# Two expert layers: 32-row transposes for the gathered rows, and heavy and light expert pairs in another order

## What is computed

```python
def hier_moe(h, w_rg, b_rg, w_re, b_re, w_g, w_u, w_d):
    ...
    g_prob = jax.nn.softmax((x @ w_rg + b_rg).astype(F32), axis=-1)
    g_p, g_i = lax.top_k(g_prob, 1)
    ...
    e_v, e_i = lax.top_k(e_sel, MOE_TOPK)
    gate = jax.nn.softmax(e_v, axis=-1) * g_p
    expert = g_i * MOE_PER_GROUP + e_i
    combine = jnp.sum(jax.nn.one_hot(expert, N_EXPERTS, dtype=F32) * gate[..., None], axis=1)
    hid = jax.nn.silu(jnp.einsum('nd,edf->nef', x, w_g)) * jnp.einsum('nd,edf->nef', x, w_u)
    hid = hid * combine[:, :, None].astype(hid.dtype)
    y = hid.reshape(B * T, N_EXPERTS * D_EXPERT) @ w_d.reshape(N_EXPERTS * D_EXPERT, D)
```

## Time and profile before

| | |
|---|---|
| three runs | 1136.48, 1138.15, 1139.21 us; median 1138.15 |
| the profiled execution | 1136.14 us, of which the traced span is 1134.3 us |
| PE busy | 1002.4 us (88%) |
| DVE, ACT, POOL busy | 520.5, 207.2, 123.0 us |
| chain that ended last | PE 70%, DMA 17%, DVE 5% |
| mean granted PE clock | 0.903 |
| moved by DMA | 304.67 MB, mean 269 GB/s |
| first expert loop | about 289 to 580 us |
| second expert loop | about 808 to 1097 us |

### The profile page before, as it was taken

How to read it: one execution, slowest core, us unless ns; L and a number is a source line. 1 busy time by engine, 2 the same in 40 slices (tenths; PEclk the granted TensorE clock), 3 DMA queues, 4 the chain that set the end, 5 groups by cost and what they waited for, 6 DMA issues and landing times.

```text
span 1134.3 us, 17810 instructions
## 1 busy us (share of the span) xinstructions
PE 1002.4 (88%) x6824; PEld 602.0 (53%) x6824; DVE 520.5 (46%) x1237; ACT 207.2 (18%) x428; POOL 123.0 (11%) x196
## 2 busy tenths in 40 slices
PE   3799999998999999988788988896899999988960
PEld 1355455453766667654544565344567666655630
DVE  1356442245354454434445557245444545532454
ACT  2223232121111111101122134011111111101111
POOL 2300111203110100100001000200201001000000
PEclk9899999997899999898979999996798999987795
DMA  9962445758787669999999440204867777999931
GB/s 313 368 250 75 156 151 198 290 183 348 276 325 296 275 238 386 420 418 419 417 385 347 145 139 7 79 19 161 350 261 290 297 297 305 418 420 419 419 132 55
DMA packets 78198, 304.67 MB, mean 269 GB/s; under 512 B 11512, under 2 KB 11824, under 8 KB 52648
## 3 DMA queue, kind: packets, MB, share of 16 engines
q1 hardware_dynamic: 66072, 277.08, 62.4%
q0 software_dynamic: 10768, 21.78, 5.6%
q10 hardware_dynamic: 1280, 4.72, 1.1%
HBM read 317.10 MB, written 5.32 MB: 284 GB/s over the span
## 4 chain that ended last, share of the span: by engine, by line
PE 70%; DMA 17%; DVE 5%; SPq 3%; ACT 2%; issue 1%; POOL 0%; ACTq 0%; DVEq 0%
PE psum L723 15%; DMA ring<-in_w_exp_up 13%; PE psum L1060 13%; PE psum L1014 11%; PE psum L1025 7%; PE psum L1082 5%; PE psum L795 4%; PE psum L921 4%; SPq L444 3%; PE psum L747 2%; DMA ring<-in_w_in_odd 2%; DMA ring<-in_w_mod 2%; PE psum L969 1%; PE psum L1191 1%; PE psum L819 1%
## 5 line engine op out<-in xcount | busy, mean ns | idle before, releaser
L1874 DVE TENSOR_TENSOR ht<-ht,psum 128x512 f32<-128x512 f32 x276 | 172.9, 681 | 173.0 <-PE psum L1025 172.8
L1060 PE MATMUL psum<-ring,arena 128*32 128x256 f32 x2816 | 174.7, 404 | 32.2 <-DMA ring<-in_w_exp_up 16.0
L1014 PEld LDWEIGHTS psum<-ident,arena 128*128 128x128 f32 x736 | 178.4, 334 | 23.0 <-issue 23.0
L1014 PE MATMUL psum<-ident,arena 128*128 128x64 f32 x736 | 185.1, 407 | 3.2 <-issue 3.2
L723 PE MATMUL psum<-ring,ht 128*128 128x512 f32 (+1 forms) x432 | 168.9, 548 | 3.4 <-ACT ht L1259 2.7
L1060 PEld LDWEIGHTS psum<-ring,arena 128*32 128x32 f32 x2816 | 96.2, 117 | 123.7 <-issue 54.2
L723 PEld LDWEIGHTS psum<-ring,ht 128*128 128x128 f32 x432 | 80.8, 190 | 84.3 <-issue 76.3
L1082 PE MATMUL psum<-ring,arena 128*32 128x512 f32 x704 | 93.8, 654 | 0.0
L1025 PE MATMUL psum<-y_top,to_token 64*128 64x512 f32 x276 | 89.5, 580 | 4.1 <-DVE y_low L1910 4.0
L1025 PE MATMUL psum<-y_low,to_token 64*128 64x512 f32 x276 | 78.8, 513 | 0.0
L1901 DVE TENSOR_TENSOR arena<-arena,psum 64x256 f32<-64x256 f32 x44 | 18.2, 413 | 123.6 <-ACT arena L1405 123.6
(11 more groups left out here) (319 smaller groups left out, 906.0 us busy)
## 6 DMA issues: line engine op xcount, KB each, us to landing
ring<-in_w_exp_gate SPq DMA_DIRECT2D x32, 2048.0 KB, 14.4
ring<-in_w_exp_up SPq DMA_DIRECT2D x32, 2048.0 KB, 16.9
ring<-in_w_exp_down SPq DMA_DIRECT2D x32, 2048.0 KB
ring<-in_w_mod SPq DMA_DIRECT2D x24, 2048.0 KB, 16.9
ring<-in_w_in_even SPq DMA_DIRECT2D x5, 2048.0 KB, 21.6
shift_scale<-mod_rows POOLq DMA_DIRECT2D x3, 2048.0 KB, 11.3
ring<-in_w_in_odd SPq DMA_DIRECT2D x3, 2048.0 KB, 20.0
ring<-in_w_out_even SPq DMA_DIRECT2D x2, 2048.0 KB, 8.9
```

The lines of the kernel that those rows point to most:

```text
L1014: t = pe.matmul(psum[:, 0, 2 * SLOTS * k:2 * SLOTS * (k + 1)], XS[v][:, k:D:KC], both_sides, start=True, stop=True)
L1060: mm = pe.matmul(psum[to:to + SLOTS, 2, 0:256], XT[:, k, SLOTS * e:SLOTS * (e + 1)], RG[:, 3 * u + a, e, k, :], start=(k == 0), stop=(k == ...
L1874: dve.tensor_tensor(acc, acc, bank(BACK_BANKS[c]), ALU.add).then_inc(M("added"), 1)
```

## The change

Four edits:

* **Transposes.** `turn_rows` uses, instead of 8 ordinary products of 128 rows with a 128 x 64 selection of the identity, 16 transposes of 32 rows each: for each of 8 column sets one transpose for rows 0 to 31 into bank 0 and one for rows 96 to 127 into bank 1 (`X_BANKS`). The input tile has its two experts apart, and `x_copy` reads two half banks.
* **Banks.** Since bank 1 is taken, `BACK_BANKS` becomes (6, 3, 7, 5, 6, 3): block 2 of `combine` writes the banks of block 0. Its first product now waits for addition 0, its second for addition 1, and VectorE does additions 0 and 1 ahead of the copy of the hidden transposes. Two waits at the start of the attention layer follow.
* **Table.** `in_slot` is written with both sides beside one another (128 columns instead of 64), so each table needs six products instead of twelve.
* **Order.** `IN_TURN` orders the pairs: two heavy, then four times a light and a heavy, then six light. VectorE computes table columns and the order of the pairs accordingly.

```diff
+IN_TURN = [True, True] + [False, True] * (HEAVY - 2) + [False] * (LIGHT - HEAVY + 2)
+PASS_LIST = [(place, part, heavy) for place, heavy in enumerate(IN_TURN) for part in range(1 + heavy)]
...
-BACK_BANKS = (6, 3, 1, 7, 5, 6)
+BACK_BANKS = (6, 3, 7, 5, 6, 3)
+X_BANKS = (0, 1)
...
-        XT = vx(KC * 2 * SLOTS, "p (k s) -> p k s", k=KC)
+        XT = vx(KC * 2 * SLOTS, "p (e k s) -> p e k s", e=2, k=KC)
...
-                    for side in range(2):
-                        rows = slice(2 * SLOTS * side, 2 * SLOTS * (side + 1))
-                        mm = pe.matmul(psum[rows, 7, 0:2 * PLACES], in_slot[:, i, :], in_pair[:, i], start=(i == 0), stop=(i == 5))
+                    mm = pe.matmul(psum[:, 7, 0:2 * PLACES], in_slot[:, i, :], in_pair[:, i], start=(i == 0), stop=(i == 5))
...
                     for k in range(KC):
-                        t = pe.matmul(psum[:, 0, 2 * SLOTS * k:2 * SLOTS * (k + 1)], XS[v][:, k:D:KC], both_sides, start=True, stop=True)
+                        for n, side in zip(X_BANKS, (slice(0, SLOTS), slice(3 * SLOTS, 4 * SLOTS))):
+                            t = pe.transpose(psum[:, n, SLOTS * k:SLOTS * (k + 1)], XS[v][side, k:D:KC], ident[side, side])
...
-                                if b == NB - 1 and part == 0 and n == 1:
-                                    pe.wait_ge(M("added"), q * 6 + 13)
+                                if b == NB - 1 and part == 0:
+                                    pe.wait_ge(M("added"), q * 6 + (13 + n))
...
-                    heavy = p < 2 * HEAVY
-                    place = p // 2 if heavy else p - HEAVY
+                    place, part, heavy = PASS_LIST[p]
                     u = place % 2
-                    new_weights = not heavy or p % 2 == 0
+                    new_weights = part == 0
...
-                    last_of_pair = p >= 2 * HEAVY or p % 2 == 1
+                    place, part, heavy = PASS_LIST[p]
+                    last_of_pair = part == int(heavy)
...
-                dve.tensor_scalar(is_heavy, rank_t, float(HEAVY), None, ALU.is_lt)
...
-                link(dve.scalar_tensor_tensor(slot_c, place_a, float(HEAVY), place_b, ALU.add, ALU.add))
+                dve.scalar_tensor_tensor(heavy_base, i64, float(PASSES - 2), h32, ALU.mult, ALU.add)
...
+                link(dve.tensor_tensor(slot_c, place_a, place_b, ALU.add))
...
-                link(dve.tensor_tensor(against, along_cols(rank), along_rows(iota16), ALU.is_equal))
+                dve.tensor_scalar(turn, rank, 2.0, -1.0, ALU.mult, ALU.add)
...
+                link(dve.tensor_tensor(against, along_cols(turn), along_rows(iota16), ALU.is_equal))
...
-                    add_half(q - 1, 0)
+                    for c in range(2):
+                        add_half(q - 1, c)
...
-                    for c in range(1, 6):
+                    for c in range(2, 6):
                         add_half(q - 1, c)
```

More of the change, by code:

```diff
@@ L117 @@
 FRONT = len(MOD_GROUPS["front"])
-MOD_BANKS = {"even": (4, 4), "gate": (0, 1), "scale": (2, 3), "norm_1": (5, 3), "router": (2, 3), "places": (2, 3), "norm_2": (2, 3),
+MOD_BANKS = {"even": (4, 4), "gate": (0, 1), "scale": (2, 3), "norm_1": (5, 3), "router": (2, 3), "places": (2, 3), "norm_2": (2, 7),
              "attention": (2, 3), "norm_3": (0, 1)}
@@ L357, in build @@
         Y_LO = rounded_at("y_low", 512)
-        in_slot = vx(6 * 2 * SLOTS, "p (i s) -> p i s", i=6)
+        in_slot = vx(6 * P, "p (i s) -> p i s", i=6)
         SGM = [vx(256, parts=2 * SLOTS) for _ in range(2)]
@@ L378, in build @@
         ef, odd, slot_p, slot_c = vx(6), vx(6), vx(6), vx(6)
-        rank_t, is_heavy, place_a, place_b = (vx(6) for _ in range(4))
+        rank_t, heavy_base, light_at, place_a, place_b = (vx(6) for _ in range(5))
+        turn, turn_tmp = vx(PAIRS), vx(PAIRS)
         n_max, n_light, n_rounds, n_tmp, n_tmp2 = vx(1), vx(1), vx(1), vx(5), vx(5)
@@ L994, in experts @@
                 for i in range(6):
-                    for side in range(2):
-                        rows = slice(2 * SLOTS * side, 2 * SLOTS * (side + 1))
-                        mm = pe.matmul(psum[rows, 5, 0:4], in_slot[:, i, :], in_first[:, i, :], start=(i == 0), stop=(i == 5))
+                    mm = pe.matmul(psum[:, 5, 0:4], in_slot[:, i, :], in_first[:, i, :], start=(i == 0), stop=(i == 5))
                 mm.then_inc(S("routing_ps"), 1)
@@ L1002, in experts @@
                 for i in range(6):
-                    for side in range(2):
-                        rows = slice(2 * SLOTS * side, 2 * SLOTS * (side + 1))
-                        mm = pe.matmul(psum[rows, 7, 0:2 * PLACES], in_slot[:, i, :], in_pair[:, i], start=(i == 0), stop=(i == 5))
+                    mm = pe.matmul(psum[:, 7, 0:2 * PLACES], in_slot[:, i, :], in_pair[:, i], start=(i == 0), stop=(i == 5))
                 mm.then_inc(S("routing_ps"), 1)
-                both_sides = ident[:, :].rearrange("p (a s) -> p a s", a=4)[:, 0:4:3, :]
                 def turn_rows(q, v):
@@ L1059, in one_pass @@
                                 to = 2 * SLOTS * (1 - a) + SLOTS * e
-                                mm = pe.matmul(psum[to:to + SLOTS, 2, 0:256], XT[:, k, SLOTS * e:SLOTS * (e + 1)], RG[:, 3 * u + a, e, k, :],
+                                mm = pe.matmul(psum[to:to + SLOTS, 2, 0:256], XT[:, e, k, :], RG[:, 3 * u + a, e, k, :],
                                                start=(k == 0), stop=(k == KC - 1))
@@ L1107, in _ @@
             mod_products(gate)
-            pe.wait_ge(S("moe0_added"), last * 6 + 14)
+            pe.wait_ge(S("moe0_added"), last * 6 + 15)
             mod_sum(gate)
@@ L1393, in x_copy @@
                     act.wait_ge(M("x_ps"), q + 1)
-                    act.copy(XT.rearrange("p k s -> p (k s)"), bank(0)).then_inc(M("x_sb"), 1)
+                    act.copy(XT.rearrange("p e k s -> p e (k s)"), psum[:, X_BANKS[0]:X_BANKS[1] + 1, 0:KC * SLOTS]).then_inc(M("x_sb"), 1)
                 def one_pass(r, p):
@@ L1791, in across @@
                     return iota[:, 0:n].rearrange("p (i n) -> p i n", i=1).broadcast_to([P, 6, n])
-                dve.tensor_tensor(in_slot, across(2 * SLOTS), along(slot_p, 2 * SLOTS), ALU.is_equal)
+                sides = [P, 6, 2, 2 * SLOTS]
+                dve.tensor_tensor(in_slot.rearrange("p i (e n) -> p i e n", e=2),
+                                  iota[:, 0:2 * SLOTS].rearrange("p (i e n) -> p i e n", i=1, e=1).broadcast_to(sides),
+                                  slot_p.rearrange("p (i e n) -> p i e n", e=1, n=1).broadcast_to(sides), ALU.is_equal)
                 link(dve.tensor_tensor(in_first, across(4), along(slot_c, 4), ALU.is_equal))
@@ L1819, in experts @@
                 link(a)
-                dve.tensor_scalar(is_heavy, rank_t, float(HEAVY), None, ALU.is_lt)
[L1821 to L1824, removed]
-                link(dve.scalar_tensor_tensor(slot_c, place_a, float(HEAVY), place_b, ALU.add, ALU.add))
+                dve.scalar_tensor_tensor(heavy_base, i64, float(PASSES - 2), h32, ALU.mult, ALU.add)
+                dve.tensor_scalar(place_a, rank_t, 3.0, -1.0, ALU.mult, ALU.add)
+                dve.tensor_scalar(place_b, rank_t, float(HEAVY), None, ALU.add)
+                link(dve.tensor_scalar(light_at, rank_t, 3.0, float(4 - 3 * HEAVY), ALU.mult, ALU.add))
+                dve.scalar_tensor_tensor(place_a, place_a, 0.0, heavy_base, ALU.max, ALU.add)
+                link(dve.tensor_tensor(place_b, light_at, place_b, ALU.min))
+                link(dve.scalar_tensor_tensor(place_b, h32, float(PASSES), place_b, ALU.mult, ALU.add))
+                link(dve.tensor_tensor(place_a, place_a, place_b, ALU.subtract))
+                link(dve.scalar_tensor_tensor(place_a, rank_t, float(HEAVY), place_a, ALU.is_lt, ALU.mult))
+                link(dve.tensor_tensor(slot_c, place_a, place_b, ALU.add))
                 dve.wait_ge(S("router_exp"), l + 1)
@@ L1863, in experts @@
                 dve.scalar_tensor_tensor(tab[:, 1, :], tab[:, 1, :], unused, tab_tmp, ALU.max, ALU.add).then_inc(S("table_ready"), 1)
-                link(dve.tensor_tensor(against, along_cols(rank), along_rows(iota16), ALU.is_equal))
+                dve.tensor_scalar(turn, rank, 2.0, -1.0, ALU.mult, ALU.add)
+                link(dve.tensor_scalar(turn_tmp, rank, 2.0, float(2 - 2 * HEAVY), ALU.mult, ALU.add))
+                link(dve.tensor_tensor(turn_tmp, turn_tmp, rank, ALU.min))
+                link(dve.scalar_tensor_tensor(turn, turn, 0.0, turn_tmp, ALU.max, ALU.subtract))
+                link(dve.scalar_tensor_tensor(turn, rank, float(HEAVY), turn, ALU.is_lt, ALU.mult))
+                link(dve.tensor_tensor(turn, turn, turn_tmp, ALU.add))
+                link(dve.tensor_tensor(against, along_cols(turn), along_rows(iota16), ALU.is_equal))
                 link(dve.tensor_tensor(against, against, along_cols(iota16), ALU.mult))
```

## The result

The changed kernel takes 1052.38 us (median of four runs, 1050.76 to 1053.32) against 1138.12 of before: a ratio of 0.9246, 95% interval 0.923 to 0.9262. The forecast was 1056 us with a range of 1044 to 1088. The profiled execution took 1052.37 us, its span 1050.5; before had 1136.14 and 1134.3.

The account below looks back on a forecast made before the run. TensorE passes bound heavy pairs and weight loads light ones, so DMA idles 38.9 and 42.6 us. Gains of 39.0 + 43.85 - 0.65 = 82.2 from 1136.14 give 1054; the median, 2.0 above, gives 1056 us, range 1044 to 1088.

Parts of the forecast that it names:

- What bounded the kernel: Expert loops: TensorE bounds heavy pairs, weight loads bound light pairs; DMA idles 38.9 and 42.6 us.
- the prediction's price for the order alone: Expert loops, first rival: passes stay at 12 us, only the new order works, 1109 us; chance 0.12.
- Turn: `turn_rows` in each pass: paired 32-row transposes take 1.3 us instead of 3.95, 2.65 less; bounds 0.9 and 3.95.
- Banks: Combine in each pass: block 2's second product waits for addition 1 instead of 0, 0.65 us more.
- The pass: One TensorE pass of the expert loops: 9.4 us at full clock, 10.1 on average with half clock kept in slow ones.
- The third rival: Expert loops: TensorE falls to half clock throughout, passes of 14.2 us, slower than before at 1170 us; chance 0.04.
- Table: Table products ahead of the loops: six full-width ones take as long as twelve paired, nothing on the path.
- Order, and what stays idle: Expert loops: with light and heavy pairs in turn DMA becomes the bound, leaving 4.5 us idle a loop.
- first load of loop 1, earlier by: First loop's start: shorter first `turn_rows` and one pass, less 0.2 of routing, issue the first load 4.55 us earlier.
- attention weights, earlier by: Behind the first loop: earlier start 4.55 plus idle time removed 34.4 bring these weights 39.0 us earlier.
- routing and start of loop 2: Second loop's first load: 2.75 and 2.0 gained, 1.0 lost to routing, so 3.75 us earlier.
- loop 2 and what follows: Second loop to the end: 38.1 idle time removed, last pass 2.0 shorter, final combine loses 0.65 us.

Follow-up runs that it names:

- the last run: The changed kernel with the 16 transposes of `turn_rows` made twice, same result: 1075.63 us, ratio 0.9399.

## Why the prediction was right

**What bounded the kernel.** Right on both parts: either edit alone moves what it should (the runs with one of the two), and the prediction's price for the order alone, 1109, was measured as 1109.87. One of the signs that it named for this did not show: the chain goes through DMA only from 455 us of the first loop on. Before that it runs through TensorE, with stretches marked "issue" that are waits for weights too: at 361.92 one of 4.54 us, which ends 0.1 us behind the landing of the up weights that SyncE issued at 348.04 (they take 18.3 us). The chain alone would not have told what bounds the loop; the run with half of each down load does.

**Turn.** 1.00 us in the chain (1.07 from the first start to the last end) against 1.3. The 16 transposes go in pairs: in the trace the two sides start 3 to 6 ns apart and the pairs 0.11 us, so the pairing taken from the 64-row products holds for 32 rows. It is nearer to the prediction's low bound, since the start and the tail take 0.15 us and not 0.3. The Trainium skill ("TensorE: Matmul & The Clock Gate", "LDWEIGHTS (loading the stationary operand)") has 0.107 us for a load of 128 columns, whatever its rows; 16 in a row would be an estimated 1.7 us, and the trace has two loads in each 0.11 us. The same page, in the table of "Why this matters for your kernels", does say that operands in different groups of 32 rows run concurrently, with starts at most 4 ns apart; that line was the one to weigh here, and the trace agrees within 2 ns.

**Banks.** 0.65 us predicted. From the start of combine to the down product the chain above has 305.66 - 302.90 = 2.76 us; before it was 11.42 - 3.45 - 3.95 - 1.85 = 2.17: 0.59 more. Weight loads of TensorE in such a pass, and VectorE at the same place:

```profile
322.47 0.18 PEld L1024 LDWEIGHTS psum<-y_top,to_token 64*128 64x128 f32 x1 [0.28 <-DVE ht L1886]
323.06 0.18 PEld L1024 LDWEIGHTS psum<-y_top,to_token 64*128 64x128 f32 x1 [0.41 <-DVE ht L1886]
...
323.73 0.16 PEld L1080 LDWEIGHTS psum<-ring,arena 128*32 128x32 f32 x8 [0.36 <-issue]
```

```profile
321.73 1.28 DVE L1886 TENSOR_TENSOR ht<-ht,psum 128x512 f32<-128x512 f32 x2 [0.69 <-PE psum L1024]
322.93 0.28 DVE L1919 COPY arena<-psum 128x128 f32<-128x128 f32 x1
323.13 2.47 DVE L1886 TENSOR_TENSOR ht<-ht,psum 128x512 f32<-128x512 f32 x4
```

The 0.16 us of the earlier trace rows is 0.28 and 0.41 now, and the copy ends 0.5 us before the down product's first load: VectorE's second addition sets the time, as argued, not the copy.

**The pass.** 9.07 us where 9.4, or 10.1 with half clock, was taken, and so just under the 9.4 to 10.5 named as a sign. 0.3 is the turn and the banks. The other 0.7 is the stretch at 0.50, which the prediction kept in half of the passes and which is gone. That is the term that was sized wrong, on the safe side. The third rival had the sign of this backwards. The Trainium skill's rule behind it ("TensorE: Matmul & The Clock Gate", Part 4: PE-mode transpose), that full clock doesn't engage for transposes, is not borne out by passes with 16 of them, which ran at 1.00 from end to end. Doubling them in the last run did bring the half clock back behind them, but the ordinary products of before had it too, so no run here shows that it matters that they are transposes.

**Table.** Nothing on the path, as predicted. TensorE at the table of the first layer:

```profile
277.06 5.38 PE L1005 MATMUL psum<-arena 128*128 128x272 f32 x12 [4.14 <-DVE arena L1850]
```

Half as many instructions, 5.38 us against 5.71.

**Order, and what stays idle.** 4.5 us a loop predicted, 2.1 and 5.8 measured. The 1 us for a new start of the queue inside the 4.5, and the 4 us for the alignment of the clock in the range's low bound, come from no row; no run shows either by itself, and the four runs of the changed kernel lie 2.6 us apart. SyncE's first loads inside the loops, as in the earlier trace rows:

```profile
302.26 0.39 SPq L453 DMA_DIRECT2D ring<-in_w_exp_gate  x1
...
781.65 0.38 SPq L453 DMA_DIRECT2D ring<-in_w_exp_gate  x1
```

The chain behind the first loop and the attention layer's first row (answering to the earlier trace rows); the granted clock behind that wait, first of before, then of the changed kernel; and TensorE's timeline at the second layer's router:

```profile
535.15 21.01 DMA ring<-in_w_in_odd
556.20 1.99 PE psum L696 x8
...
558.94 8.50 PE psum L727 x16
```

```profile
597.10:640.00 42.90, 40.19 (x110) 18.70 (x111) 24.62 (x42) 9.98 (x24) 5.08 (x8) 1.00 0.79 277
556.20:599.10 42.90, 40.22 (x105) 18.89 (x106) 21.25 (x38) 9.48 (x23) 5.06 (x8) 0.94 0.76 270
```

```profile
735.56 2.70 PE L973 MATMUL psum<-arena,ht 128*128 128x36 f32 x13 [0.88 <-DVE ht L1528]
```

| step | predicted, us | measured, us |
|---|---|---|
| first load of loop 1, earlier by (part of the next step) | 4.55 | 306.43 - 302.26 = 4.2 |
| attention weights, earlier by | 39.0 | 597.05 - 556.16 = 40.9 |
| attention layer, to the second router | 0 | 2.1 lost (38.8 earlier at 735.56) |
| routing and start of loop 2 | 3.75 | 43.53 - 38.76 = 4.8 |
| loop 2 and what follows | 38.1 + 2.0 - 0.65 = 39.45 | 309.1 - 268.85 = 40.3 |
| sum | 82.2 | 83.8 |

The one step that is not in the prediction is the loss in between. Weights are last at the attention layer as predicted, but TensorE now waits 3.5 us for them in place of 2.08, and over the first 42.9 us behind the wait the granted clock is 0.94 where it was 1.00 before. Its first transposes take 1.99 us in place of 1.16, and the 16 product instructions behind them 8.50 in place of 7.10: these two make 2.2 us, all of the loss. The norm's last vector operation ends 43.2 us earlier (553.2 against 596.43) and the weights land 40.9 earlier, so the wait grew; that the clock fell because of it is read from the order of events and was not tried. The 1.0 us more at the start of loop 2 is mostly its first pass, from gate and up to gate and up 10.60 us in place of 13.57: 2.97 less where 2.0 was taken, 0.6 of it in its gate and up products (4.99 in place of 5.59).

That the second loop idles more than the first is nothing new: the two differ by 3.7 us in both kernels.

Between the profiled executions the sum was right to 1.6 us, partly by luck, because two misses partly cancel: the steps around the loops gave 3.7 us more than predicted (1.9, 1.0 and 0.8), and the attention layer took 2.1 back. The forecast lies 3.6 us above the median, as it added 2.0 for the median of before over its profiled execution, and in the changed kernel the two agree.

## What to carry to other kernels

Look at the DMA rate over slices before looking at engines: two levels in one loop say that two kinds of work with opposite limits stand one behind the other, and putting them in turn is worth the idle time of the lower level, but no more than that, and a faster pass draws on the same account. Price two edits that fill the same gap together, not as a sum: here 68 and 29 us made 86. And when a long run of small products on TensorE is cut, look at the granted clock of the work behind it, since that can add to the gain: in the last run, the other way round, the clock doubled the price of the longer turn (16 us where the turn alone explains 8).

## What the runs showed of the hardware

- Transposes of 32 rows in different row groups run as pairs 3 to 6 ns apart, one pair each 0.11 us (16 in 1.00 us); two sides one after the other still overlap in part (16 in 1.47 us).
- The half clock behind `turn_rows` came with a longer turn, not with a longer pass: absent with 1.00 us in passes of 9.07 and 9.81, present with 1.47 in every second pass and with 1.88 in two of four.
- The stream kept 415 GB/s as a mean over 222 us of the first loop and 408 over as much of the second, with gathers, loads and a TensorE at work in 188 of them, so the mix costs the prediction's 419 little.
